# A decoder layer on eight cores: the order of tiles 4 and 5 and of two page loads, and the last output unit cut in two

## What is computed

```python
h = rmsnorm(x, norm_pre[l])
proj = jnp.einsum('bsd,de->bse', h, w_in[l])
xa, ga, u, vb, gb, q, gc = split_cols(proj, IN_SPLITS)
ya = pool_mixer(xa, pool_w[l], pool_scale[l]) * jax.nn.silu(ga)
yb = spatial_gating(u, vb, ...) * jax.nn.silu(gb)      # layernorm(vb), 128x128 mixing
yc = memory_cross_attention(q, k_m, v_m) * jax.nn.silu(gc)
y = jnp.concatenate([rmsnorm(ya, g_a), rmsnorm(yb, g_b), rmsnorm(yc, g_c)], axis=-1)
out = jnp.einsum('bse,ed->bsd', y, w_out[l])
x = x + rmsnorm(out, norm_post[l])
```

## Time and profile before

| | |
|---|---|
| three runs | 1257.91, 1259.50, 1259.72 us; median 1259.5 |
| the profiled execution | 1258.87 us |
| its span, slowest core (3) | 1257.2 us |
| spans of the other cores | 1251.3 (core 2) to 1256.9 (core 0) |
| PE busy | 1220.3 us, 97% |
| DVE, ACT, POOL busy | 488.0, 475.9, 216.0 us |
| chain that ended last | PE 90%, DMA 3%, DVE 2%, ACT 2%, issue 1% |

### The profile page before, as it was taken

One profiled execution on the slowest core, in us unless ns is written; L12 is line 12 of the kernel. 1 busy time (PEld: TensorE's weight loads), 2 busy tenths in 40 slices (PEclk: granted clock), 3 DMA queues, 4 the chain that ended last, 5 costly groups with the idle time before them and its releaser, 6 DMA issues.

```text
span 1257.2 us, 17843 instructions; the slowest of 8 cores (1251.3 to 1257.2 us)
## 1 busy us (share of the span) xinstructions
PE 1220.3 (97%) x6224; PEld 582.0 (46%) x6224; DVE 488.0 (39%) x782; ACT 475.9 (38%) x892; POOL 216.0 (17%) x205
## 2 busy tenths in 40 slices
PE   6889999999999999999999999999989999999997
PEld 3345544444444455555554444444434444444443
DVE  4167624332232233444443233333222454343434
ACT  4377733422222232222225555555632232223222
POOL 1000001221211011111121111111222222222222
PEclk9999999999999999999999999999999999999999
DMA  9945322554234452645435541441975492533231
GB/s 210 245 152 173 69 81 68 105 90 83 50 67 81 83 93 45 107 88 91 97 63 98 86 82 34 81 88 34 178 212 138 129 307 75 178 133 118 93 109 68
DMA packets 50938, 137.83 MB, mean 110 GB/s; under 512 B 22785, under 2 KB 35201, under 8 KB 37137
## 3 DMA queue, kind: packets, MB, share of 16 engines
q0 software_dynamic: 7632, 50.86, 24.3%
q1 hardware_dynamic: 43218, 85.83, 21.3%
HBM read 153.39 MB, written 29.36 MB: 145 GB/s over the span
## 4 chain that ended last, share of the span: by engine, by line
PE 90%; DMA 3%; DVE 2%; ACT 2%; issue 1%; SPq 0%; DVEq 0%; POOLq 0%; POOL 0%; ACTq 0%
PE ps L279 89%; DMA mem_pages<-x 2%; DMA mem_pages<-y_scr 2%; PE ps L282 1%; ACT mem_pages L391 1%; DVE mem_pages L395 1%; DVE mem_pages L1155 0%; ACT mem_pages L1030 0%; SPq L291 0%; ACT L1030 0%; DVE stat L1025 0%; DVE mem_pages L1127 0%; DVE mem_pages L1035 0%; DVE mem_pages L545 0%; ACT stat L256 0%
## 5 line engine op out<-in xcount | busy, mean ns | idle before, releaser
L279 PE MATMUL ps<-mem_pages 128*128 128x512 bf16 (+2 forms) x5760 | 1195.7, 369 | 7.9 <-DMA mem_pages<-y_scr 4.0
L279 PEld LDWEIGHTS ps<-mem_pages 128*128 128x128 bf16 x5760 | 555.7, 98 | 630.5 <-issue 22.8
L713 POOL TENSOR_TENSOR mem_pages<-mem_pages 128x512 f32<-128x512 f32 x72 | 91.1, 1266 | 599.9 <-ACT mem_pages L706 597.3
L700 ACT ACTIVATE mem_pages<-mem_pages,small_c 128x512 bf16<-128x512 f32 x96 | 68.8, 716 | 275.4 <-DVE mem_pages L772 148.1
L1127 DVE SCALAR_TENSOR_TENSOR mem_pages<-ps,stat,mem_pages 128x512 f32<-128x512 f32 x128 | 96.0, 750 | 166.8 <-PE ps L279 144.4
L1135 POOL TENSOR_TENSOR mem_pages<-mem_pages 128x512 f32<-128x512 f32 x64 | 81.1, 1267 | 257.3 <-ACT jk L1132 257.3
L1132 ACT ACTIVATE jk<-mem_pages 128x512 bf16<-128x512 f32 x64 | 40.3, 629 | 224.0 <-DVE mem_pages L1127 224.0
L903 DVE TENSOR_TENSOR mem_pages<-mem_pages 128x526 f32<-128x526 f32 (+3 forms) x80 | 56.1, 701 | 100.8 <-ACT mem_pages L897 95.8
L762 DVE TENSOR_TENSOR mem_pages<-ps,mem_pages 128x512 f32<-128x512 f32 x32 | 22.1, 691 | 141.3 <-PE ps L279 141.3
L732 ACT ACTIVATE mem_pages<-ps 128x512 f32<-128x512 f32 x96 | 54.5, 590 | 22.8 <-PE ps L279 19.4
L748 DVE CAST mem_pages<-ps 128x512 bf16<-128x512 f32 (+1 forms) x24 | 14.4, 601 | 124.6 <-PE ps L279 121.4
(11 more groups left out here) (66 smaller groups left out, 422.9 us busy)
## 6 DMA issues: line engine op xcount, KB each, us to landing
mem_pages<-w_pages POOLq DMA_DIRECT2D x44, 1024.0 KB, 12.9
mem_pages<-x SPq DMA_DIRECT2D x32, 1024.0 KB, 7.8
out<-mem_pages SPq DMA_DIRECT2D x15, 1024.0 KB, 4.7
y_scr<-mem_pages SPq DMA_DIRECT2D x96, 128.0 KB, 1.9
mem_pages<-y_scr SPq DMA_DIRECT2D x12, 1024.0 KB, 14.6
mem_pages<-w_pages POOLq DMA_DIRECT2D x8, 512.0 KB, 19.7
mem_pages<-mem SPq DMA_DIRECT2D x2, 1024.0 KB, 6.2
mem_pages<-mem_norm SPq DMA_DIRECT2D x1, 1024.0 KB
```

What stands on the lines that cost most here:

```text
L279: return lambda e: e.matmul(out, lhsT=lhsT, rhs=rhs, start=start, stop=stop)
L700: P.op("act", lambda e: e.activation(out=yv, in_=tmp, func=AF.Copy, scale=gbr[:, c:c + 1]), reads=[tmp_b[i], gbr_b], writes=[ring_b[r]])
L713: P.op("pool", lambda e: e.tensor_tensor(out=accl_v if last else acc, in0=acc, in1=dst, op=ALU.add), reads=[dst_b, acc_b[tb]], writes=[acc ...
```

## The change

In the head, `x_load(4)` waits for the first half of weight page ("v", 0, 0) instead of that of ("v", 0, 1). `x_a(4)` is emitted ahead of the `v_ln_half(tt, 0)`, which come later in two pairs; `x_a(5)` is emitted behind the second transposes of tile 4, ahead of all `v_ln_half(tt, 1)`; and the parts of `v_mm(3, 1, ...)` are spread between the others.

In `out_q`, `y_load(0)` (from n = 12) stands ahead of `wo_load(2)` (from n = 13); `gp_load` stays last.

In the last tile, unit (15, 3) becomes two of 256 columns with five partial sums in new columns of `stat`; the final multiply-add of the second quarter is made by ACT (scale) and POOL (add), those of the others by DVE, and the stores go out in the order first, third, second, fourth quarter.

```diff
--- before.py
+++ after.py
@@ -247,6 +247,7 @@
     ST_SSX, ST_RSX, ST_VS, ST_VQ, ST_VM, ST_VR, ST_VT = 0, 20, 40, 56, 72, 88, 104
     ST_RBR, ST_MX, ST_NB, ST_RI, ST_RS, ST_SO, ST_FO, ST_FR = 120, 168, 176, 184, 192, 256, 320, 336
     ST_LH0, ST_LH1 = 352, 360
+    ST_SL = 368
     ST_EPS = 383
 
     def sc(i):
@@ -546,7 +547,7 @@
                                               scalar2=sc(ST_VR + tt), op0=ALU.add, op1=ALU.mult),
              reads=[bank[b], bank[b + 1], s1], writes=[vn_b[tt]])
 
-    W2, W3, W4 = wbuf(("v", 0, 1)), wbuf(("v", 1, 0)), wbuf(("v", 1, 1))
+    W1, W4 = wbuf(("v", 0, 0)), wbuf(("v", 1, 1))
     x_a(0)
     x_a(1)
     x_a(2)
@@ -554,7 +555,7 @@
     x_pe(1, halves=(0,))
     x_a(3)
     x_pe(2, halves=(0,))
-    x_load(4, [W2[0].wtok])
+    x_load(4, [W1[0].wtok])
     x_load(5, [W4[0].wtok])
     x_load(6, [W4[1].wtok])
     x_load(7)
@@ -574,9 +575,9 @@
     for part in range(2):
         for tt in range(4):
             v_mm(tt, 0, 1, part)
-            if part == 1:
-                v_ln_half(tt, 0)
     x_a(4)
+    for tt in range(2):
+        v_ln_half(tt, 0)
     drop(*VN, dyn=False)
     take(*VN)
     vn_b += [nbuf("vn%d" % tt, VN[tt // 4]) for tt in range(NTT)]
@@ -584,19 +585,18 @@
         for tt in range(3):
             v_mm(tt, 1, 0, part)
     x_pe(4, (7, 7), (0,))
+    for tt in range(2, 4):
+        v_ln_half(tt, 0)
     v_mm(0, 1, 1, 0)
     v_mm(1, 1, 1, 0)
     x_pe(4, (7, 7), (1,))
+    x_a(5)
     v_mm(2, 1, 1, 0)
-    v_mm(3, 1, 0, 0)
-    v_mm(3, 1, 0, 1)
     for tt in range(3):
+        v_mm(3, 1, tt // 2, tt % 2)
         v_mm(tt, 1, 1, 1)
         v_ln_half(tt, 1)
         v_ln_end(tt)
-        if tt == 1:
-            x_a(5)
-    v_mm(3, 1, 1, 0)
     v_mm(3, 1, 1, 1)
     v_ln_half(3, 1)
     v_ln_end(3)
@@ -1099,7 +1099,7 @@
 
     def take_orow(tt):
         p = dyn()
-        orow[tt] = (p, [nbuf("or%d_%d" % (tt, db), p) for db in range(4)], nbuf("orr%d" % tt, p))
+        orow[tt] = (p, [nbuf("or%d_%d" % (tt, db), p) for db in range(5)], nbuf("orr%d" % tt, p))
 
     def load_xres(tt):
         p = dyn()
@@ -1107,55 +1107,67 @@
         dma_sp(page_f(p), x_d[tt * 128:(tt + 1) * 128, :], writes=[b], sem="d_ps%d" % p)
         xres[tt] = (p, b)
 
-    def wo_unit(tt, db):
+    def wo_unit(tt, db, lo=0, n=512, so=None):
         tb = tt // 4
+        so = ST_SO + tt * 4 + db if so is None else so
         p, obs, _ = orow[tt]
-        ov = page_f(p)[:, db * 512:(db + 1) * 512]
+        ob = obs[db + (1 if lo else 0)]
+        c0 = db * 512 + lo
+        ov = page_f(p)[:, c0:c0 + n]
         bks = []
         for br in range(3):
             b = balloc()
             yv = page_bf(ypage[(tb, br)][0]).rearrange("p (c t) -> p c t", c=8)
             Wo = w8(("wo", db, br))
-            fns = [mm(psb(b), yv[:, q, (tt % 4) * 128:(tt % 4 + 1) * 128], Wo[:, q, :], q == 0, q == 7)
+            fns = [mm(psb(b, 0, n), yv[:, q, (tt % 4) * 128:(tt % 4 + 1) * 128], Wo[:, q, lo:lo + n], q == 0, q == 7)
                    for q in range(8)]
             P.group("pe", fns, reads=[ypage[(tb, br)][1], wbuf(("wo", db, br))], writes=[bank[b]])
             bks.append(b)
         rc = ST_RBR + tt
-        P.op("act", lambda e: e.activation(out=ov, in_=psb(bks[0]), func=AF.Identity, scale=sc(rc)),
-             reads=[bank[bks[0]], rbr_b[tb]], writes=[obs[db]])
+        P.op("act", lambda e: e.activation(out=ov, in_=psb(bks[0], 0, n), func=AF.Identity, scale=sc(rc)),
+             reads=[bank[bks[0]], rbr_b[tb]], writes=[ob])
         for br in (1, 2):
             P.op("dve", lambda e, br=br: e.scalar_tensor_tensor(
-                out=ov, in0=psb(bks[br]), scalar=sc(rc + br * 16), in1=ov, op0=ALU.mult, op1=ALU.add),
-                reads=[bank[bks[br]], rbr_b[tb], obs[db]], writes=[obs[db]])
+                out=ov, in0=psb(bks[br], 0, n), scalar=sc(rc + br * 16), in1=ov, op0=ALU.mult, op1=ALU.add),
+                reads=[bank[bks[br]], rbr_b[tb], ob], writes=[ob])
         bfree(*bks)
-        so = ST_SO + tt * 4 + db
-        P.op("act", lambda e: e.activation(out=jk_v, in_=ov, func=AF.Square, scale=D ** -0.5, accum_out=sc(so)),
-             reads=[obs[db]], writes=[jk_b, so_b[tt]])
-        gv = page_f(gp["p"])[:, db * 512:(db + 1) * 512]
+        P.op("act", lambda e: e.activation(out=jk_v[:, 0:n], in_=ov, func=AF.Square, scale=D ** -0.5,
+                                           accum_out=sc(so)),
+             reads=[ob], writes=[jk_b, so_b[tt]])
+        gv = page_f(gp["p"])[:, c0:c0 + n]
         P.op("pool", lambda e: e.tensor_tensor(out=ov, in0=ov, in1=gv, op=ALU.mult),
-             reads=[obs[db], gp["b"]], writes=[obs[db]])
+             reads=[ob, gp["b"]], writes=[ob])
 
     so_b = [Buf("so%d" % t) for t in range(NTT)]
 
     def wo_final(tt, last=False):
         p, obs, _ = orow[tt]
         stf = Buf("stf")
-        c0 = ST_SO + tt * 4
-        P.op("dve", lambda e: e.reduce_sum(out=sc(ST_FO + tt), in_=stat[:, c0:c0 + 4], axis=AX.X),
+        c0, cn = (ST_SL, 5) if last else (ST_SO + tt * 4, 4)
+        P.op("dve", lambda e: e.reduce_sum(out=sc(ST_FO + tt), in_=stat[:, c0:c0 + cn], axis=AX.X),
              reads=[so_b[tt]], writes=[stf])
         rstd_of(sc(ST_FR + tt), sc(ST_FO + tt), stf)
         xp, xb = xres[tt]
-        n = 4 if last else 1
-        w = 2048 // n
         rows = out_d[tt * 128:(tt + 1) * 128, :]
-        for q in range(n):
-            o = page_f(p)[:, q * w:(q + 1) * w]
-            xv = page_f(xp)[:, q * w:(q + 1) * w]
-            ob = obs if n == 1 else [obs[q]]
-            P.op("dve", lambda e, o=o, xv=xv: e.scalar_tensor_tensor(out=o, in0=o, scalar=sc(ST_FR + tt), in1=xv,
-                                                                     op0=ALU.mult, op1=ALU.add),
+        pieces = [(0, 4, "dve", obs)]
+        if last:
+            pieces = [(1, 1, "pool", [obs[1]]), (0, 1, "dve", [obs[0]]), (2, 1, "dve", [obs[2]]),
+                      (3, 1, "dve", [obs[3], obs[4]])]
+        for i, (q, n, eng, ob) in enumerate(pieces):
+            o = page_f(p)[:, q * 512:(q + n) * 512]
+            xv = page_f(xp)[:, q * 512:(q + n) * 512]
+            if eng == "pool":
+                P.op("act", lambda e, o=o: e.activation(out=o, in_=o, func=AF.Identity, scale=sc(ST_FR + tt)),
+                     reads=[stf] + ob, writes=ob)
+                P.op("pool", lambda e, o=o, xv=xv: e.tensor_tensor(out=o, in0=o, in1=xv, op=ALU.add),
+                     reads=[xb] + ob, writes=ob)
+                continue
+            P.op(eng, lambda e, o=o, xv=xv: e.scalar_tensor_tensor(out=o, in0=o, scalar=sc(ST_FR + tt), in1=xv,
+                                                                   op0=ALU.mult, op1=ALU.add),
                  reads=[stf, xb] + ob, writes=ob)
-            dma_sp(rows[:, q * w:(q + 1) * w], o, reads=ob, sem="d_o%d_%d" % (tt % 4, q))
+        for i, (q, n, eng, ob) in enumerate(pieces[1:3] + pieces[0:1] + pieces[3:] if last else pieces):
+            dma_sp(rows[:, q * 512:(q + n) * 512], page_f(p)[:, q * 512:(q + n) * 512], reads=ob,
+                   sem="d_o%d_%d" % (tt % 4, i))
         drop(p, xp)
         orow.pop(tt)
         xres.pop(tt)
@@ -1165,8 +1177,8 @@
         gp["b"] = nbuf("gpost", gp["p"])
         dma_sp(page_f(gp["p"]), norm_post_d.partition_broadcast(128), writes=[gp["b"]], sem="d_g")
 
-    out_q = [(3, 0, lambda: wo_load(0)), (3, 0, lambda: wo_load(1)), (3, 0, lambda: wo_load(2)),
-             (3, 13, lambda: y_load(0)), (2, 0, gp_load)]
+    out_q = [(3, 0, lambda: wo_load(0)), (3, 0, lambda: wo_load(1)), (3, 12, lambda: y_load(0)),
+             (3, 13, lambda: wo_load(2)), (2, 0, gp_load)]
 
     for n in range(len(blocks)):
         hh, tb = blocks[n]
@@ -1226,9 +1238,13 @@
         if tt % 4 == 0 and tt // 4 + 1 < 4:
             y_load(tt // 4 + 1)
         take_orow(tt)
-        for db in range(4):
-            wo_unit(tt, db)
-        wo_final(tt, last=tt == NTT - 1)
+        last = tt == NTT - 1
+        for db in range(3 if last else 4):
+            wo_unit(tt, db, so=ST_SL + db if last else None)
+        if last:
+            wo_unit(tt, 3, 0, 256, ST_SL + 3)
+            wo_unit(tt, 3, 256, 256, ST_SL + 4)
+        wo_final(tt, last)
         if tt + 2 < NTT:
             load_xres(tt + 2)
         if tt % 4 == 3:
```

## The result

The changed kernel takes 1267.82 us (median; 1266.95 to 1268.93), the kernel before beside it 1259.03 us: a ratio of 1.0071, 95% interval 1.0054 to 1.0089. Slower, as forecast, but by 8.8 us instead of 5.2, and just outside the range.

A forecast was written before the change was run, and what follows sets the result against it. PE was taken as the bound, busy 97% of the span, so only its idle or half-clock places pay. Head -0.3, middle +5.5 (3.7 + 1.8) and tail 0.0 gave +5.2 on 1258.87: 1264.1 us, range 1257 to 1267.

The forecast's parts named there:

- Head, forecast -0.3 us: Head: three removed PE stalls collapse into one before tile 4's first product; -0.3 us, between +2.5 and -2.
- PE starts tile 4 at T + 8.0: Head: T is when ACT's wait for tile 5's load ends, 56.8; PE's first tile 4 product follows at 64.8.
- Branch results, gain 5.7 us: Output stage start: loading tiles 0 to 3 earlier removes 4.0 us of PE waits and 1.7 of half clock.
- The gain page, forecast 925.6 and the flush at 929.9: Output stage: post-norm gain load lands late beside weight pages, at 925.6; PE's ss flush waits until 929.9, 3.7 later than before.
- the other cores share issue order and waits; those that lose less today at 916 end up at the same place: Sum: the forecast worked out on core 3, by the per-core view the slowest, was taken to hold for all cores.
- Half clock behind the long wait, forecast +1.8: After the ss flush: PE's 9.4 us idle brings a half-clock stretch, costing +1.8 us.
- Tail, forecast 0.0 between +0.3 and -1.0: Last tile: statistics 0.4 us earlier, eaten by +0.4 if DVE pieces and POOL's add exclude each other; 0.0.
- I add nothing: Sum: the runs' median lies 0.6 us above the profiled execution; no allowance made for it in the forecast time.
- (1): Output stage: gain page in time, by 916.3, so the middle gives its 5.7 us; 1252.9 us, chance 0.10.
- (2): Output stage: gain page lands in between, 918.4 to 922; 1255.1 at 918.4, 1259.5 at 921; chance 0.15.
- (3): Head turns dear: tile 5 lands two microseconds later, or longer half clock, adds 2.5; 1266.6 us, chance 0.10.
- (4): Head keeps PE at full clock and tile 5's load comes earlier, middle as forecast; 1262 us, chance 0.05.

## Why the prediction was right and wrong

**Head, forecast -0.3 us: right.** The step "PE starts tile 4 at T + 8.0" holds on every core (8.02 to 8.04), with T between 56.05 and 57.81 (forecast 56.8), and the part alone measured no difference. The half clock behind the stall was a little short: 16 matmuls took 5.0 to 6.5 us, forecast 5.4. Against the spread of T it does not count. What I did not see is how cheap the remedy was; the runs with tile 5 later or its load earlier gave 7 us.

**Branch results, gain 5.7 us: right.** The run with the gain page early is 0.45% (0.3 to 0.6) faster, which is 5.7 us.

**The gain page, forecast 925.6 and the flush at 929.9: the mechanism right, the core wrong.** The changed kernel has the gain multiply between 922.5 and 927.9, the mean of the eight cores 925.4; the flush between 926.5 and 931.9, mean 929.4. The forecast is the mean, and the metric is the slowest core. The failed step is "the other cores share issue order and waits; those that lose less today at 916 end up at the same place". Before, the cores' flushes lay within 5.5 us of each other and core 3 was next to the latest, so it was a fair stand-in for the slowest. Afterwards PE waits for a transfer at the same place, each core's transfer crawls by its own measure, and core 3 is among the early ones (926.57, against 931.93 on core 6). On core 3 itself the change cost 2.8 us and not 5.2: the gain multiply there started 3.2 us ahead of the forecast. The forecast lets the last weight page land 23.3 us after its issue, as before; it took 21.2 us on core 3 and 24.5 on core 6. The 3.8 us from there to the gain page measured 2.6 to 4.7 on the eight cores, so that pattern held. A term that hangs on a landing should have been carried with the spread of that landing over the cores, which was there to be read before: the spread of the third flush (921.3 to 926.9) came from landings too. This term is 2.0 of the 3.0 us by which the profiled span exceeded the forecast; 0.3 lie behind the flush, 0.4 in the tail, and 0.3 are the head's gain, which the sum takes off although the 929.9 is worked out without it.

**Half clock behind the long wait, forecast +1.8: small by 0.3 on core 6.** From the flush to PE's last matmul it took 324.0 us there and 321.9 in the kernel before on core 3. On the eight cores this stretch grew by 1.2 to 3.0 us.

**Tail, forecast 0.0 between +0.3 and -1.0: wrong, outside its bounds.** The lock between DVE and POOL is as forecast: 1.75 us for the piece beside the add, 0.74 otherwise. The Trainium skill, "SBUF — State Buffer", section "Who interferes with whom", states that lock, and the trace agrees. DVE was through 0.3 us earlier after PE's last matmul than before, 5.36 against 5.66. The failed step is unspoken: that the end of the span is set by the last store. It was, by 0.5 us at the least. With POOL's add put there it is set by POOL's close, 4.65 us after the add: from the slowest core before to the slowest after +0.4 (9.04 to 9.47), in the mean +0.9, and in the part alone 0.11%. No row of before shows the 4.65 us at work, but its rows could have warned: they show no program that ends less than 5.1 us after POOL's last instruction. POOL's add ends 4.8 us after PE's last matmul, so an end 9.0 us after it left 4.2 for the close: an unknown cost, and I gave it no bound.

The median of the runs lies 0.9 us above the profiled execution's 1266.95 us; with "I add nothing" this carried the time over the range's edge: 1266.95 lies inside 1267, by 0.05 us, and 1267.82 outside. Which side it fell on was luck; the 2.9 us between 1264.1 and 1266.95 are the terms above. Of the rivals, (1) is excluded on all eight cores, and (2), a page between 918.4 and 922, missed by a little on two: it landed at 922.2 and 922.3 on cores 0 and 3, on the other six at 924.4 to 927.6. (3) came in part: on cores 1 and 2 the head is 1.5 and 1.9 us later than before, but the head alone shows no loss. (4) did not happen.

**What stays open:** why the last of the same three weight pages takes 21.6 us on some cores and up to 24.7 on others (the kernel with the new order alone), and not always on the same cores. The gain page follows it, but no run here varied what the cores share. Open too is whether the gain page would be in time with the weight pages beside it if it stood ahead of the two stores.

## What to carry to other kernels

When a load moves in a queue, follow every later transfer that will pass beside it, and what stands ahead of that one in its queue, to whoever waits for it and whoever stands behind that one; the saving and the loss here are the same size and lie in neighbouring entries of one list. When the end of a wait is a landing, carry the spread over the cores and take its late end, since the slowest core is the metric. Let GpSimd finish early at the end of a program: here work taken off VectorE and given to it there had to be worth a closing time of 4.65 us.

## What the runs showed of the hardware

- The end of the program came no earlier than 4.64 us after POOL's last instruction, on all 40 core traces in which POOL works after the last statistics (4.64 to 4.78 us). ACT's last instruction could end 1.8 us before it.
- A 1 MB load from SP, behind two stores of 128 KB, took 6.6 us from issue to landing without weight pages of POOL beside it and 16 to 21 us with them. The stores ahead of it moved in 1 KB packets, as many as the 8 KB packets of the weights (32 and 32 in 2 us, 0.03 MB against 0.26 MB), and took 13.3 and 16.7 us instead of 4. The Trainium skill, "DMA: Bandwidth & Descriptors", section "Queues, rings and completion order", has the turn by turn of packets. That packets and not bytes are shared evenly is what makes small ones dear here.
- DVE and POOL, both with SBUF operands, can hold each other up in one pass: 1751 ns instead of 737 for DVE's piece and 1.69 us instead of 1.27 for POOL's add. Without the halves POOL's add began just ahead of DVE's piece and kept its 1.26 us, and only that piece was long, 1798 ns. With them it began while a piece of DVE ran: the add was long, and so was DVE's next piece. Who comes first decides who waits.
